# A two-block model in one kernel: tile 0 first at three norm boundaries, another order in attention 2, and the second layer's memory keys in two halves

## The reference, cut to what matters

```python
for i in range(2):
    h = rms_norm(x, norm_mix_pre[i])
    mem_n = rms_norm(mem, mem_norm[i])
    if i == 0:   # dilated band attention, 12 heads of 64, and memory attention, 4 heads of 64
        mixed = attention(h, mem_n, att_w_in, att_w_out, rel_bias, mem_w_kv[0])
    else:        # gated deltanet, 6 heads of 128, conv of 5 taps, both directions, and memory attention
        mixed = deltanet(h, mem_n, dn_w_in, dn_conv, ..., dn_w_out, mem_w_kv[1])
    x = x + rms_norm(mixed, norm_mix_post[i])
    h = rms_norm(x, norm_ffn_pre[i])
    gate, up = split(h @ ffn_w_gate_up[i])          # 1024 -> 2 * 2816
    x = x + rms_norm((silu(gate) * up) @ ffn_w_down[i], norm_ffn_post[i])
```

## Time and profile before

| | us |
|---|---|
| median of 3 runs | 2118.93 |
| lowest and highest run | 2118.62, 2124.21 |
| the profiled execution, device time | 2123.88 |
| its span on the core | 2122.1 |
| PE busy (matmul) in it | 1897.2, 89% |
| DVE busy, ACT busy | 578.1, 418.0 |
| chain of waits: PE, DMA, DVE, ACT | 73%, 16%, 5%, 3% |

### The profile page before, as it was taken

The page is one execution under the profiler, slowest core; times in us unless marked ns, Lnnn a source line. Parts: engine busy times, 40 slices in busy tenths (PEclk is TensorE's granted clock), DMA queues, the critical chain, the costliest instruction groups (busy, mean ns, idle before and its releaser), DMA issues.

```text
span 2122.1 us, 24580 instructions
## 1 busy us (share of the span) xinstructions
PE 1897.2 (89%) x9817; PEld 1052.5 (50%) x9818; DVE 578.1 (27%) x1149; ACT 418.0 (20%) x638; POOL 61.2 (3%) x82
## 2 busy tenths in 40 slices
PE   6999997899998878889878769989999999999998
PEld 4744452233333222223222228649884677768863
DVE  4666242211221112212221132330000389520001
ACT  2230122121222121112212121330000334220000
POOL 2000010000000000000000010002001000000000
PEclk9999988999999899999999889999999999999999
DMA  9646678999999999999999994184430323074420
GB/s 313 233 160 253 215 265 351 428 428 386 418 427 428 427 429 428 427 419 384 427 428 427 428 408 154 39 299 120 157 140 10 135 80 130 4 285 157 143 77 20
DMA packets 107773, 577.54 MB, mean 272 GB/s; under 512 B 7283, under 2 KB 8815, under 8 KB 83100
## 3 DMA queue, kind: packets, MB, share of 16 engines
q1 hardware_dynamic: 103548, 566.54, 66.7%
q0 software_dynamic: 4160, 10.06, 1.7%
HBM read 575.50 MB, written 4.22 MB: 273 GB/s over the span
## 4 chain that ended last, share of the span: by engine, by line
PE 73%; DMA 16%; DVE 5%; ACT 3%; issue 2%; DVEq 0%; SPq 0%; ACTq 0%
DMA ring<-in_w_up 13%; PE ps L2085 13%; PE ps L1475 10%; PE ps L2091 7%; PE ps L1510 5%; PE ps L719 5%; PE ps L1489 3%; PE ps L1522 3%; PE ps L904 2%; PE ps L1499 2%; PE ps L2064 2%; PE ps L2200 1%; PE ps L2675 1%; PE ps L1029 1%; PE ps L1100 1%
## 5 line engine op out<-in xcount | busy, mean ns | idle before, releaser
L2085 PE MATMUL ps<-arena,ring 128*128 128x256 f32 x1280 | 276.6, 379 | 0.0
L2085 PEld LDWEIGHTS ps<-arena,ring 128*128 128x128 f32 x1280 | 243.0, 190 | 33.0
L1510 PE MATMUL ps<-ring,arena 128*32 128x512 f32 x1216 | 164.7, 690 | 59.3 <-DMA ring<-in_w_up 59.2
L1475 PE MATMUL ps<-ring,arena 128*64 128x512 f32 x960 | 213.1, 595 | 0.0
L2091 PE MATMUL ps<-ring,arena 128*128 128x512 f32 x352 | 151.4, 592 | 0.0
L719 PE MATMUL ps<-arena,ring 128*128 128x256 f32 x608 | 132.9, 380 | 0.0
L1475 PEld LDWEIGHTS ps<-ring,arena 128*64 128x64 f32 x960 | 66.1, 137 | 134.3 <-issue 133.8
L1510 PEld LDWEIGHTS ps<-ring,arena 128*32 128x32 f32 x1216 | 39.6, 124 | 170.4 <-issue 100.9
L719 PEld LDWEIGHTS ps<-arena,ring 128*128 128x128 f32 x608 | 115.1, 190 | 17.0 <-issue 1.6
L1489 PE MATMUL ps<-ring,arena 128*64 128x512 f32 x480 | 106.3, 594 | 11.2 <-ACT arena L1438 11.2
L2091 PEld LDWEIGHTS ps<-ring,arena 128*128 128x128 f32 x352 | 66.9, 190 | 83.3 <-issue 83.2
(11 more groups left out here) (614 smaller groups left out, 2070.3 us busy)
## 6 DMA issues: line engine op xcount, KB each, us to landing
ring<-in_w_gate SPq DMA_DIRECT2D x64, 2048.0 KB, 18.5
ring<-in_w_up SPq DMA_DIRECT2D x64, 2048.0 KB, 22.0
ring<-in_w_down SPq DMA_DIRECT2D x64, 2048.0 KB, 19.0
ring<-in_ffn_w_gate_up SPq DMA_DIRECT2D x22, 2048.0 KB, 8.1
ring<-in_ada_w SPq DMA_DIRECT2D x12, 2048.0 KB, 16.4
ring<-in_ffn_w_down SPq DMA_DIRECT2D x10, 2048.0 KB, 7.8
ring<-in_w_in SPq DMA_DIRECT2D x8, 2048.0 KB, 21.5
ring<-in_dn_w_in SPq DMA_DIRECT2D x6, 2048.0 KB, 7.7
```

What stands on the lines that cost most here:

```text
L1475: m = pe.matmul(bank(b)[c * CAP:(c + 1) * CAP, :], xT[:, j * P + h * CAP:j * P + (h + 1) * CAP], w[h][:, j, c * 512:(c + 1) * 512], start= ...
L1510: m = pe.matmul(bank(b)[(2 * i + c) * FEW:(2 * i + c + 1) * FEW, :], xT[:, j * P + h * CAP:j * P + h * CAP + FEW], w[h][:, j, c * 512:(c + ...
L2085: m = pe.matmul(bank(b0 + g)[:, c * SEQ:(c + 1) * SEQ], w[:, k, (2 * g + c) * P:(2 * g + c + 1) * P], hT2[:, k, :], start=(k == 0), stop=( ...
```

## The change

The boundaries q = 1, 2, 3: PE turns tile 0 in the midst of tile 1's last projection (after half of the last output block in attention 2 and deltanet; before the last down piece in the first feed-forward layer), and ACT and DVE copy tile 0's turned banks before they go to tile 1. After the projection PE goes straight to products of tile 0: both first gate/up pieces are now split by tile, and in the deltanet layer the gates, all memory queries and the first column projection; tile 1 is turned in between. In both feed-forward layers down pieces 2 to 5 instead of 4 and 5 are done for tile 0 and then for tile 1.

Attention 2: the first column projection comes before the memory scores, the memory probabilities after the third; other PSUM banks are used (6, 4, 0 for the columns, 2 and 3 for the value rows), and the waits follow them. DVE copies the values of units 6, 7 and 8 one by one between other steps.

The second layer's memory keys: the first half stays ahead of the norm, the second half stands just before the memory scores in bank 4 with its own ACT copy. Their weight piece goes from the first to the second place of attention 2's pieces.

The diff, with unchanged lines left out and indents halved:

```diff
@@ -245,7 +245,7 @@
-      return piece(by_k(A["mem_w_kv_2"][i], 0, 2 * MW), mkv_ps, 2 * i + 2)
+      return piece(by_k(A["mem_w_kv_2"][i], 0, 2 * MW), mkv_ps, 3 * i + 2)
@@ -1117,7 +1117,7 @@
-      if c:
+      if c or i:
@@ -1845,12 +1845,12 @@
-        if t:
-          act_first_turned(act, o, q)
...
+        if t == 0:
+          act_first_turned(act, o, q)
@@ -1866,13 +1866,13 @@
-        if t:
-          dve_turned_on(dve, o, q, 0, 1)
...
+        if t == 0:
+          dve_turned_on(dve, o, q, 0, 1)
@@ -1902,7 +1902,7 @@
-        o(act.copy(kvKept[:, 0:512], bank(3)), mkv_ready)
+        o(act.copy(kvKept[:, 0:256], bank(3)[:, 0:256]), mkv_ready)
@@ -1985,10 +1985,11 @@
-        pc_mem.append(mem_piece(1))
...
-        pc_at.extend(piece(by_k(w, n * 512, n * 512 + 512), proj_ps, 5 + i_) for i_, n in enumerate((4, 0, 1, 2, 3)))
+        for i_, n in enumerate((4, 0, 1, 2, 3)):
+          pc_at.append(piece(by_k(w, n * 512, n * 512 + 512), proj_ps, 5 + i_))
+          if i_ == 0:
+            pc_mem.append(mem_piece(1))
@@ -2056,24 +2057,30 @@
-      w = arrived(pe, pc_gu[i][0])
-      def first_gate_up(g, t):
+      w0, w1 = arrived(pe, pc_gu[i][0]), arrived(pe, pc_gu[i][1])
+      def gate_up(n, w, g, t):
...
-            m = pe.matmul(bank(4 + g)[:, c * SEQ + t * P:c * SEQ + (t + 1) * P], w[:, k, (2 * g + c) * P:(2 * g + c + 1) * P],
+            m = pe.matmul(bank(4 + 2 * n + g)[:, c * SEQ + t * P:c * SEQ + (t + 1) * P], w[:, k, (2 * g + c) * P:(2 * g + c + 1) * P],
...
-      pe_over(pe, q, (0,))
...
-      first_gate_up(0, 0)
+      gate_up(0, w0, 0, 0)
+      gate_up(0, w0, 1, 0)
+      if i == 0:
+        gate_up(1, w1, 0, 0)
...
-      first_gate_up(1, 0)
+      if i == 1:
+        gate_up(1, w1, 0, 0)
+      gate_up(1, w1, 1, 0)
...
-      first_gate_up(0, 1)
-      first_gate_up(1, 1).then_inc(gu_ps, 1)
+      gate_up(0, w0, 0, 1)
+      gate_up(0, w0, 1, 1).then_inc(gu_ps, 1)
+      gate_up(1, w1, 0, 1)
+      gate_up(1, w1, 1, 1).then_inc(gu_ps, 1)
...
-        if n == 0:
+        if n < 2:
@@ -2091,7 +2098,7 @@
-      for n, pc in enumerate(pc_dn[i][:4]):
+      for n, pc in enumerate(pc_dn[i][:2]):
@@ -2099,7 +2106,7 @@
-      last = [(n, arrived(pe, pc_dn[i][n])) for n in (4, 5)]
+      last = [(n, arrived(pe, pc_dn[i][n])) for n in range(2, 6)]
@@ -2107,6 +2114,8 @@
+            if (i, n) == (0, 4):
+              pe_over(pe, 2, (0,))
@@ -2141,10 +2150,12 @@
-      pool.wait_ge(mkv_ps, 4)
+      pool.wait_ge(mkv_ps, 5)
...
+    QK_BANK = (6, 4, 0)
@@ -2152,8 +2163,7 @@
-      for c in range(2):
-        pe_mem_keys(pe, 1, 3, c)
+      pe_mem_keys(pe, 1, 3, 0)
@@ -2164,24 +2174,24 @@
+      pe_cols(pe, arrived(pe, pc_at[1]), QK_BANK[0], hT2, KD, proj_ps)
...
+      pe_mem_keys(pe, 1, 4, 1)
...
-      pe_cols(pe, arrived(pe, pc_at[1]), 6, hT2, KD, proj_ps)
+      pe.wait_ge(mkv_ready, 5)
+      pe_cols(pe, arrived(pe, pc_at[2]), QK_BANK[1], hT2, KD, proj_ps)
...
-      pe_cols(pe, arrived(pe, pc_at[2]), 0, hT2, KD, proj_ps)
-      pe.wait_ge(proj_ev, 7)
+      pe_cols(pe, arrived(pe, pc_at[3]), QK_BANK[2], hT2, KD, proj_ps)
+      pe.wait_ge(proj_ev, 8)
...
-      pe.wait_ge(sc_sub, 6)
-      pe_cols(pe, arrived(pe, pc_at[3]), 2, hT2, KD, proj_ps)
-      pe.wait_ge(proj_ev, 8)
-      pe_rows(pe, arrived(pe, pc_at[4]), (0, 1), hT2, KD, proj_ps)
-      pe.wait_ge(proj_ev, 10)
+      pe_rows(pe, arrived(pe, pc_at[4]), (2, 3), hT2, KD, proj_ps)
+      pe.wait_ge(proj_ev, 9)
...
-        if n < 8:
-          pe.wait_ge(sc_sub, n - 1)
-        else:
+        if n == 7:
+          pe.wait_ge(proj_ev, 10)
+        elif n > 7:
@@ -2191,7 +2201,7 @@
-      pe.wait_ge(mkv_ready, 5)
+      pe.wait_ge(mkv_ready, 6)
@@ -2226,7 +2236,9 @@
-      out_of(1, 1, 0, KD).then_inc(out_ps, 1)
+      out_of(1, 1, 0, KD // 2)
+      pe_over(pe, 1, (0,))
+      out_of(1, 1, KD // 2, KD).then_inc(out_ps, 1)
@@ -2235,20 +2247,21 @@
-        o(act.copy(qkA[:, 4 * n:4 * n + 4, :].rearrange("p c s -> p (c s)"), bank((6, 0, 2)[n], 2)), proj_ev)
+        o(act.copy(qkA[:, 4 * n:4 * n + 4, :].rearrange("p c s -> p (c s)"), bank(QK_BANK[n], 2)), proj_ev)
...
+      act.wait_ge(mkv_ps, 4)
+      o(act.copy(kvKept[:, 256:512], bank(4)[:, 256:512]), mkv_ready)
...
-      qk(0)
-      qk(1)
+      for n in range(3):
+        qk(n)
...
-      qk(2)
...
-      o(act.copy(vA[:, :, 0:512], bank(0, 2).rearrange("p (t n) -> p t n", t=TT)), proj_ev)
+      o(act.copy(vA[:, :, 0:512], bank(2, 2).rearrange("p (t n) -> p t n", t=TT)), proj_ev)
@@ -2263,7 +2276,7 @@
-      act.wait_ge(mkv_ps, 4)
+      act.wait_ge(mkv_ps, 5)
@@ -2315,9 +2328,9 @@
-      def outs(t):
-        for g in range(3):
-          dve_pv(dve, o, None, 6 + 3 * t + g, yA[:, 2 * g:2 * g + 2, t * P:(t + 1) * P])
+      def values_out(n):
+        t, g = (n - 6) // 3, (n - 6) % 3
+        dve_pv(dve, o, None, n, yA[:, 2 * g:2 * g + 2, t * P:(t + 1) * P])
@@ -2332,12 +2345,15 @@
+      values_out(6)
...
+      values_out(7)
...
-      outs(0)
+      values_out(8)
...
-      outs(1)
+      for n in (9, 10, 11):
+        values_out(n)
@@ -2426,7 +2442,7 @@
-      pool.wait_ge(mkv_ready, 6)
+      pool.wait_ge(mkv_ready, 7)
@@ -2459,20 +2475,29 @@
-      pe_over(pe, 2, (0,))
+      def first_cols(c0, c1, t):
+        for c in range(c0, c1):
+          for k in range(KD):
+            m = pe.matmul(bank(4 + c // 2)[:, (c % 2) * SEQ + t * P:(c % 2) * SEQ + (t + 1) * P], w1[:, k, c * P:(c + 1) * P],
+                   hT2[:, k, t * P:(t + 1) * P], start=(k == 0), stop=(k == KD - 1))
+        return m
...
+      memory_queries(1, 0)
+      w1 = arrived(pe, pc_dw[1])
+      first_cols(0, 2, 0)
...
-      memory_queries(1, 0)
+      first_cols(2, 4, 0)
...
+      first_cols(0, 2, 1)
...
-      pe.wait_ge(mkv_ready, 6)
+      pe.wait_ge(mkv_ready, 7)
...
-      pe_cols(pe, arrived(pe, pc_dw[1]), 4, hT2, KD, proj_ps)
+      first_cols(2, 4, 1).then_inc(proj_ps, 1)
@@ -2670,8 +2695,8 @@
-      def out_of(t, i, w):
-        for k in range(KD):
+      def out_of(t, i, w, k0=0, k1=KD):
+        for k in range(k0, k1):
@@ -2720,8 +2745,10 @@
-      for i, w in enumerate(ws):
-        out_of(1, i, w).then_inc(out_ps, 1)
+      out_of(1, 0, ws[0]).then_inc(out_ps, 1)
+      out_of(1, 1, ws[1], 0, KD // 2)
+      pe_over(pe, 3, (0,))
+      out_of(1, 1, ws[1], KD // 2, KD).then_inc(out_ps, 1)
...

```

## The result

| us | before | after |
|---|---|---|
| median | 2119.77 (4 runs) | 2100.84 (4 runs) |
| lowest and highest run | 2118.62, 2124.21 | 2098.03, 2105.14 |
| profiled execution, its span | 2123.88, 2122.1 | 2105.14, 2103.4 |
| mean granted clock of TensorE | 0.949 | 0.956 |

The time after is 0.9912 of the time before, with a 95% interval of 0.9894 to 0.9930: 18.9 us faster where 20.4 were forecast, at 2100.84 against 2098.5. That is inside the range of 2093 to 2109. The sum came close partly because two terms that were too large met one of 1.65 us that the forecast had at nothing and that was luck.

What follows compares the result with a forecast made beforehand. PE's chain of waits was taken as the bound: idles at three boundaries, then half clock. Gains 0.2 + 2.45 + 2.5 + 6.1 + 4.0 + 5.1 = 20.4 us took the median 2118.93 to 2098.5, range 2093 to 2109.

Steps and rivals of the forecast that it cites:

- norm, keys, projections: Second layer's norm and attention 2's projections: 0.2 us from a narrower key copy, 2.45 us from two idles gone.
- values, first output projection: Attention 2: projection starts 1.1 to 2.5 us earlier, its weight piece landing sooner; gain 2.5 us, bounds 1.1 and 4.2.
- FFN boundary 0: First feed-forward boundary, from turning to the second gate/up piece's end: 38.3 us become 32.2, gain 6.1.
- deltanet, to DVE's L2901: Deltanet boundary: DVE's 3.98 us idle goes, 0.4 come back; DVE resumes 4.0 us sooner, bounds 3 and 6.
- FFN 1 boundary: Second feed-forward boundary: 37.2 us become 32.2, gain 5.1, low bound 4; 7.2 us of PE work cover tile 1's 7.0.
- The third rival: Split gate/up pieces: the 192 extra weight loads are exposed; 2135 us, or 2119 by the skill's 107 ns; chances 0.03 and 0.02.
- The second (a cover fails): One boundary: a piece or diagonal is late, the clock falls again, 4 to 6 us given back; 2103 us, chance 0.2.
- The fourth: Rival: idles are re-created one wait later, the turned tile waiting for something else; about 2116 us, chance 0.02.
- the clock may still fall: First output projection: 8.62 us against 6.9 at full clock; an idle of 2 us stays, so 2.5 us gain was taken.
- the first rival: Deltanet stage follows PE's full 7.5 us instead of DVE's chain: 3.4 us more gain, 2095 us, chance 0.08.
- Most of that is hidden: Deltanet: memory scores start 3.6 us after the queries instead of 0.96, yet only 0.4 us come back.
- the lead of the down pieces: Feed-forward down pieces: tile 0's lead grows from 12 to 28 products where 7 us are needed; worth 0.

Runs made afterwards that it cites:

- e_one: Changed kernel with only the first gate/up piece split by tile in both feed-forward layers, the second whole behind tile 1's turning; 837.49 us after the expert loop (changed kernel 840.00).
- e_late: Changed kernel, but tile 0 is turned right behind tile 1's last projection at all three boundaries, no longer inside it; median 2105.27 us, 0.9924 of before.
- The filler: Changed kernel plus nine unread 128-column products in PE's 2.07 us idle before unit 8's values; 837.16 us after the expert loop (changed kernel 840.00).
- e_keys: Changed kernel with both halves of the second layer's memory keys ahead of the first norm again; 840.69 us after the expert loop (changed kernel 840.00).
- e_table: Changed kernel plus a one-element dummy exponential on ACT behind the deltanet gate logarithm, asking for the table early; 840.90 us after the expert loop (changed kernel 840.00).
- b_two: Changed kernel plus early exponential table, memory scores one block nearer, 9 fillers before unit 8's values, 28 before the key products; both pieces split; median 2090.61 us, 0.9861 of before.

## Why the prediction was right or wrong

| term | forecast | measured | mark |
|---|---|---|---|
| norm, keys, projections | 0.2 + 2.45 | 2.51 | A |
| values, first output projection | 2.5 (1.1 to 4.2) | 0.93 | B |
| FFN boundary 0 | 6.1 | 6.18 | C |
| deltanet, to DVE's L2901 | 4.0 (3 to 6) | 3.10 | E |
| FFN 1 boundary | 5.1 | 4.91 | in F |
| the clock's phase in the rest of the deltanet | 0 | 1.65 | in F |
| FFN 0, FFN 1, expert loop | 0 | -0.13, -0.04, -0.41 | D, G |
| sum | 20.4 | 18.7 | |

**Right, and for the reason given:** the two FFN boundaries and the projections. They rested on one number, the spacing of the split instructions, and on no cover failing. The spacing is the 112 ns that the earlier trace rows showed, on 256 instructions. The rule that speaks against the edit (the Trainium skill, "TensorE: Matmul & The Clock Gate", "LDWEIGHTS (loading the stationary operand)", with "The mechanism") does not hold here: with an estimated 107 ns per exposed load, the 160 instructions would have needed twice their 17.87 us. The third rival falls with it. The second (a cover fails) had its best place at FFN 1, and the cover there was used up to within 0.1 us; e_one, which takes away another cover, that of tile 1's copies behind the turning, shows what a missing cover costs: 0.94 us of idle at once. The fourth didn't occur: e_late has the re-created wait that it meant, and it is 1.0 us where the idle had been 3.7.

**Wrong in size: values and the first output projection.** The step that failed is "the clock may still fall ... I take 2.5, nearer to a fall that comes again". I had the fall, but with the loss read before, 8.62 us, as if it didn't depend on when the projection starts. The start is 1.67 us earlier by its distance to unit 6's scores (26.93 against 28.60), within my 1.1 to 2.5. But the clock is low for 6.8 us in both traces, and the projection now starts 1.5 us earlier in that stretch (2.3 us into it instead of 3.8). So 1.5 us more of it run at half speed, which costs 0.75 us; it takes 0.74 us longer, and 1.67 - 0.74 = 0.93. Of the 1.57 us missing, 0.83 are the start and 0.74 the clock. The lower bound of 1.1 was no bound, since it held only the earliest start and let the clock cost no more than before. The filler and e_keys show the other end, 3.83 and 3.35 us of gain against before.

**Wrong in size: the deltanet stage.** The reasoning held in its main step. PE came 7.6 us sooner and DVE did not follow, which ends the first rival. The step that failed is "Most of that is hidden, since ACT's exponential of them starts at 1691.20 ..., behind ACT's own gate functions". The exponential has a table load of 1.28 us ahead of it, and I left out that this load stands behind ACT's wait. Before, it ran while the scores were already there; now ACT waits 1.58 us first and loads then. So 3.98 us of idle go, 1.55 come back at the exponential instead of 0.4, 0.54 are gained at the key activation (L2525 starts 1.63 us after the convolutions, L2500 2.17), and 0.15 at the 24 instructions (4.69 against 4.84): 3.98 - 1.55 + 0.54 + 0.15 = 3.12, and 3.10 are measured. e_table moves the 1.27 us at ACT as this says.

**Luck:** 1.65 us in F. One group of 36 instructions of 128 columns, which no edit touches, took 5.90 us before (at 1817.96, the granted clock at 0.50 until 1821.4) and 4.29 after (at 1805.74, the clock at 1.00). It took 5.89 to 5.91 in ten other kernels of the table and 4.29 in two, e_one and b_two. With the instruction count of after, no other kernel is under 175.8 in F. Without it the change gives about 17.5 us after the loop in a profiled execution. The medians, 18.9 apart with an interval of some 4 us either way, can't tell 17.5 from 19.

**Not counted:** the lead of the down pieces, called worth 0, carries 0.8 us once the turning is placed earlier.

## What to carry to other kernels

Price an edit by the spacing of the same instruction in the trace, and add up stage by stage from marks that both traces have: here an untouched loop moves by 15 us between executions, while the touched stages repeat to 0.1. When work is pulled ahead of an engine, look at what that engine must do between the end of its wait and its first result (a table load, a half clock) and put it ahead of the wait. An idle of 2 us on PE can cost a second 2 to 3 us in what follows it; where nothing useful fits, a few products that nobody reads are worth trying; those of 128 columns paid here, and the granted clock afterwards shows whether they did.
